# A two-block transformer kernel: attention steps, borders between stages, and the norm between two layers

## The reference

```python
for i in range(2):                                   # first block ("A")
    x = x + hybrid_mixer(rmsnorm(x, norm1_g[i]), w_in[i], ...) @ w_out[i]
    x = x + conv_glu_ffn(rmsnorm(x, norm2_g[i]), w_up[i], conv_w[i], conv_b[i], w_down[i])
x = rmsnorm(x, final_g)
for l in range(2):                                   # second block ("B")
    mod = (silu(c) @ ada_w[l] + ada_b[l]).reshape(b, 3, 3, 1024)   # shift, scale, gate of 3 sub-layers
    y = swiglu(x * (1 + scale0) + shift0, ffn_w13[l, 0], ffn_w2[l, 0])
    x = layer_norm(ALPHA * x + 0.5 * (1 + gate0) * y, ln_g[l, 0], ln_b[l, 0])
    y = token_mixer(x * (1 + scale1) + shift1, w_in[l], w_out[l], ...)
    x = layer_norm(ALPHA * x + (1 + gate1) * y, ln_g[l, 1], ln_b[l, 1])
    y = swiglu(x * (1 + scale2) + shift2, ffn_w13[l, 1], ffn_w2[l, 1])
    x = layer_norm(ALPHA * x + 0.5 * (1 + gate2) * y, ln_g[l, 2], ln_b[l, 2])
```

## Time and profile before

| | |
|---|---|
| median of 3 runs | 1954.8 us (1954.37 to 1962.56) |
| profiled execution | 1956.14 us |
| its span | 1954.3 us |
| PE busy | 1859.0 us (95%), 12538 matmuls |
| DVE busy | 1357.1 us (69%) |
| ACT busy | 956.5 us (49%) |
| POOL busy | 98.9 us (5%) |
| mean granted TensorE clock | 0.984 |
| chain of work that ended last | PE 85%, DVE 8%, ACT 5%, issue 2%, DMA 1% |

### The profile page before, as it was taken

One profiled execution on the slowest core, in us unless ns is written; L12 is line 12 of the kernel. 1 busy time (PEld: TensorE's weight loads), 2 busy tenths in 40 slices (PEclk: granted clock), 3 DMA queues, 4 the chain that ended last, 5 costly groups with the idle time before them and its releaser, 6 DMA issues.

```text
span 1954.3 us, 31245 instructions
## 1 busy us (share of the span) xinstructions
PE 1859.0 (95%) x12538; PEld 1705.4 (87%) x12538; DVE 1357.1 (69%) x2149; ACT 956.5 (49%) x1421; POOL 98.9 (5%) x104
## 2 busy tenths in 40 slices
PE   7989999899899989999998999998999999999997
PEld 5878999788799989998987989997999888979997
DVE  4576878647678876677777777677666777865445
ACT  5665444556644455434655354435343664444432
POOL 0000000000000000000002201100000001400100
PEclk9999999899999999999999999998999999999999
DMA  7215777431377767774530257775775432035552
GB/s 268 80 64 198 297 278 271 177 118 66 130 268 292 278 234 282 279 278 174 180 123 23 93 212 285 285 277 211 293 283 200 153 131 85 1 130 195 194 204 76
DMA packets 54509, 374.42 MB, mean 192 GB/s; under 512 B 6016, under 2 KB 6656, under 8 KB 12800
## 3 DMA queue, kind: packets, MB, share of 16 engines
q1 hardware_dynamic: 51536, 361.98, 50.2%
q0 software_dynamic: 2304, 9.93, 1.4%
q10 hardware_dynamic: 560, 0.99, 0.2%
HBM read 371.83 MB, written 1.05 MB: 191 GB/s over the span
## 4 chain that ended last, share of the span: by engine, by line
PE 85%; DVE 8%; ACT 5%; issue 2%; DMA 1%; SPq 0%; ACTq 0%; DVEq 0%
PE bank L688 13%; PE bank L690 13%; PE bank L689 13%; PE bank L837 6%; PE bank L838 6%; PE bank L839 6%; PE bank L754 3%; PE bank L755 3%; PE bank L756 3%; DVE w_lo L1911 2%; PE bank L1297 2%; PE bank L1307 1%; ACT w_hi L1395 1%; PE bank L799 1%; PE bank L800 1%
## 5 line engine op out<-in xcount | busy, mean ns | idle before, releaser
L1911 DVE TENSOR_TENSOR w_lo<-raw,w_hi 128x2048 fp32r<-128x2048 f32 (+4 forms) x273 | 605.2, 2220 | 88.2 <-ACT w_hi L1395 88.0
L688 PE MATMUL bank<-hT_hi,w_hi 128*128 128x256 f32 x2304 | 654.1, 284 | 2.0 <-DVE scratch L2611 2.0
L689 PE MATMUL bank<-hT_lo,w_hi 128*128 128x256 f32 x2304 | 651.8, 283 | 0.0
L690 PE MATMUL bank<-hT_hi,w_lo 128*128 128x256 f32 x2304 | 651.8, 283 | 0.0
L1395 ACT ACTIVATE w_hi<-raw 128x2048 fp32r<-128x2048 f32 (+4 forms) x270 | 505.5, 1875 | 146.3 <-PE bank L839 116.2
L688 PEld LDWEIGHTS bank<-hT_hi,w_hi 128*128 128x128 f32 x2304 | 440.1, 191 | 8.9 <-issue 6.5
L689 PEld LDWEIGHTS bank<-hT_lo,w_hi 128*128 128x128 f32 x2304 | 440.2, 191 | 2.8 <-issue 0.5
L690 PEld LDWEIGHTS bank<-hT_hi,w_lo 128*128 128x128 f32 x2304 | 440.2, 191 | 0.2
L837 PE MATMUL bank<-w_hi,hid_hi 128*128 128x512 f32 x528 | 207.3, 393 | 3.8 <-DVE w_lo L1911 3.4
L838 PE MATMUL bank<-w_lo,hid_hi 128*128 128x512 f32 x528 | 206.8, 392 | 0.0
L839 PE MATMUL bank<-w_hi,hid_lo 128*128 128x512 f32 x528 | 205.9, 390 | 0.0
(11 more groups left out here) (400 smaller groups left out, 2391.7 us busy)
## 6 DMA issues: line engine op xcount, KB each, us to landing
raw<-in_wb SPq DMA_DIRECT2D x158, 1024.0 KB, 4.8
raw<-in_wa SPq DMA_DIRECT2D x94, 1024.0 KB, 4.9
scratch<-in_wm SPq DMA_DIRECT2D x72, 1024.0 KB, 7.0
raw<-in_wb SPq DMA_DIRECT2D x8, 940.0 KB, 4.5
raw<-in_wb SPq DMA_DIRECT2D x4, 936.0 KB, 4.6
lnw<-in_ln_g POOLq DMA_DIRECT2D x6, 512.0 KB, 4.5
lnw<-in_ln_b POOLq DMA_DIRECT2D x6, 512.0 KB, 5.4
scratch<-in_c SPq DMA_DIRECT2D x5, 512.0 KB, 3.7
```

Of the source, the lines that this page charges most:

```text
L688: nc.tensor.matmul(out, ah, bh, start=(i == 0), stop=False)
L689: nc.tensor.matmul(out, ah, bl, start=False, stop=False)
L690: last = nc.tensor.matmul(out, al, bh, start=False, stop=(i == n - 1))
L1911: return nc.vector.tensor_tensor(w_lo[:, slot, cols], raw[:, raw_slot, cols], w_hi[:, slot, cols].bitcast(F32), ALU.subtract)
```

## The change

It has three parts.

**B's attention steps.** The first matrices of heads 4 and 5 are joined into one set of double width (`FIRST`) and moved from behind `systems` into attention steps 3, 4 and 5. Scores of the first two units wait only for the system matrix of heads 4 and 5; the wait on the token features moves to the first values. The denominators of the mLSTM norm (three small instructions) stand in step 10, and the wide multiply (128x768) behind the last output, no longer in step n = 3 of the inverse loop. The low part of chunk `wout` + 1 is made in four quarters: two between the last outputs, two behind the multiply.

**A's borders.** At the start of each layer of A tiles are split by halves of k: k 0 to 3 of both rows, chunk 1's high and low part, and then k 4 to 7. At the border from layer 0 to layer 1 ACT makes chunk 1's high part first, DVE adds the last sum first, and row 0's transposes stand ahead of the sweep's last product. The last piece of `ada` of A's FFN goes behind the last feature. The high part of chunk `A_WIN` (first of the output projection) is made in quarters on ACT in attention steps 9 to 12, its low part on DVE in step 20. Row 1 of the second norm and of the final norm is written in two halves, with a wait for each.

**B's border.** Between B's two layers row 0 and row 1 are only normalized, as between sub-layers. Gain and bias of that norm go into layer 1's first modulation (three more 128x8 instructions on DVE), and eight POOL instructions (128x512) put them on x during layer 1's first FFN.

The diff, cut to its core:

```diff
 # PE
+                            if (i, half, f) == (1, 1, FT - 1) and turn_first is not None:
+                                turn_first()
...
-                pe.wait_ge(A["xn"], due(A, "xn", 2 * TT))
-                turn_tile(A, xn, 1, 2)
-                ffn(A, split + (A_WIN + A_WOUT), FT * l, 2)
+                turn_tile(A, xn, 1, 2, lambda bank: pe.wait_ge(A["xn"], due(A, "xn", 2 * TT + bank)))
+                ffn(A, split + (A_WIN + A_WOUT), FT * l, 2, turn_first=turn_next if l + 1 < DEPTH else None)
...
-                    turn_row(i, lambda half, i=i: pe.wait_ge(FIN["x"], TT * l + i + 1))
+                    if l == 0:
+                        turn_row(i, lambda half, i=i: pe.wait_ge(FIN["x"], TT) if i and half else pe.wait_ge(FIN[("x", "x_half")[i]], 1))
+                    else:
+                        turn_row(i, lambda half, i=i: pe.wait_ge(EDGE[f"nx{i}"], half + 1))
...
-                    if 2 <= u < MOBA_H + 2:
+                    if u < 2:
+                        pe.wait_ge(B["dmul"], due(B, "dmul", GDN_H - 1 + u))
+                    elif u < MOBA_H + 2:
...
-                pe.wait_ge(B["tm"], due(B, "tm", N_TOK))
-                pe.wait_ge(B["dmul"], due(B, "dmul", GDN_H))
 # POOL, layer 1, first FFN
+                        for j in range(8):
+                            row, i, half = j // 4, j // 2 % 2, j % 2
+                            cols = slice(half * 512, half * 512 + 512)
+                            pool.wait_ge(chunk_mm, l * B_N + S_A + NEW + 4 + 2 * j)
+                            if row:
+                                pool.wait_ge(FIN["x"], TT + j - 3)
+                            nc.gpsimd.tensor_tensor(x[:, i, cols], x[:, i, cols], lnw[:, row, cols], (ALU.mult, ALU.add)[row]
+                                                    ).then_inc(FIN["x"], 1)
 # ACT, layer 0 of A (first lines) and layer 1
-                    hi_tile(A, 0, 0, "g1")
+                    hi_tile(A, 0, 0, "g1", range(KH))
+                    hi_tile(A, 0, 1, "g1", range(KH))
+                    hi_a(1)
...
-                hi_tile(A, 0, 1, "g1")
-                hi_a(1)
+                    hi_a(1)
+                    act.wait_ge(A["x"], summed(l - 1, 1, 0))
+                    square(NEXT, 1, 0)
+                    half_mean(NEXT, 1, 6 * l + 4)
+                    hi_tile(A, 0, 0, "g1", range(0, 2))
...
+                for i in range(TT):
+                    hi_tile(A, 0, i, "g1", range(KH, KT))
...
-                hi_a(A_WIN)
+                    if 0 <= step - SPLIT_AT < 4:
+                        hi_quarter(step - SPLIT_AT)
 # DVE
+                if l:
+                    scale, shift = by_kind[:, 0, 1, :], by_kind[:, 0, 0, :]
+                    link(nc.vector.tensor_tensor(bshift[:, 0, :], sbp("ln_b")[:, 2 * KT:3 * KT], scale, ALU.mult))
+                    link(nc.vector.tensor_tensor(shift, shift, bshift[:, 0, :], ALU.add))
+                    link(nc.vector.tensor_tensor(scale, scale, sbp("ln_g")[:, 2 * KT:3 * KT], ALU.mult))
...
-                    lo_tile(A, 0, 0, "g1", range(0, 4))
                     sums(l - 1, 1, 1)
+                    lo_tile(A, 0, 0, "g1", range(0, 2))
                     plain_row(1, TT * l + 2, 2 * TT * l + 2)
-                    lo_tile(A, 0, 0, "g1", range(4, KT))
-                lo_tile(A, 0, 1, "g1")
-                for c in range(1, A_WIN - 1):
+                    lo_tile(A, 0, 0, "g1", range(2, KH))
+                    lo_a(1)
+                    lo_tile(A, 0, 1, "g1", range(KH))
+                for i in range(TT):
+                    lo_tile(A, 0, i, "g1", range(KH, KT))
+                for c in range(2, A_WIN - 1):
...
-                    dve.wait_ge(B["dmul"], due(B, "dmul", h + 1))
-                    v = xx[:, 2 * h:2 * h + 2, 1, :]
-                    link(nc.vector.tensor_tensor(v, sysT[:, h, :].rearrange("p (k n) -> p k n", n=P)[:, 0:3:2, :],
-                                                 const("lev0").unsqueeze(1).to_broadcast([P, 2, P]), ALU.mult))
-                    nc.vector.tensor_tensor(v, ident.unsqueeze(1).to_broadcast([P, 2, P]), v, ALU.subtract).then_inc(B["xinit"], 1)
-                    dve.wait_ge(B["xinit"], due(B, "xinit", h + 1))
-                    nc.vector.transpose(xx[:, 2 * h:2 * h + 2, 0, :], v).then_inc(B["xt"], 1)
+                    if h < GDN_H - 2:
+                        for part in range(3):
+                            first_matrices(h, part)
...
+                    if 0 <= step - MOBA_H + 1 < 3:
+                        first_matrices(len(FIRST) - 1, step - MOBA_H + 1)
...
+                    if step > NUB and step + 1 < NUB + B_LAGV:
+                        lo_quarter(B_S0["wout"] + 1, step - NUB - 1)
+                dve.wait_ge(B["o_ev"], due(B, "o_ev", NUB))
+                link(nc.vector.tensor_tensor(hc, hc, wide(hst2), ALU.mult))
...
-                for half in range(2):
-                    from_down(2, 1, half, split + (B_N + NEW))
-                second_statistics()
-                for i in range(TT):
-                    last_row(2, i)
+                    from_down(2, 1, 0, None)
+                    first_scale(2)
+                    from_down(2, 1, 1, split + (B_N + NEW))
+                    second_statistics()
+                    second_normal(2)
```

More of the change, by code:

```diff
@@ L450, in build @@
         V_CHUNK = max(c for c, (f, _, _) in enumerate(B_WIN) if F_LQ - 1 in f)
+        FIRST = [(h, 1) for h in range(GDN_H - 2)] + [(GDN_H - 2, 2)]
         B_LAGP, B_LAGT, B_LAGO, B_LAGV = 1, 2, 3, 4
@@ L815, in gate_on_all, with ffn @@
                                      start=True, stop=True).then_inc(B["gateb"], 1)
-            def ffn(N, split, h0, v, gate=None):
+            def ffn(N, split, h0, v, gate=None, turn_first=None):
                 def up(f, f2, pos, slot, wait_bank=True, features=None):
@@ L1621, in compressed, with hi_quarter @@
                                              ACT.Copy).then_inc(A["cpt_ev"], 1)
+                def hi_quarter(q):
+                    s_, cols = A_WIN, slice(q * CW // 4, (q + 1) * CW // 4)
+                    if q == 0:
+                        act.wait_ge(raw_in[(s_ + A_D) % RING], arrivals(l, s_ + A_D))
+                        act.wait_ge(chunk_mm, split + s_ + 1)
+                    last = nc.scalar.activation(w_hi[:, s_ % RING, cols], raw[:, (s_ + A_D) % RING, cols], ACT.Copy)
+                    if q == 3:
+                        last.then_inc(hi_done, 1)
                 for step in range(NU + LAG_T):
@@ L2022, in ffn @@
                 post(FT - 1, 1, 1, lambda: None)
+                if conv:
+                    ada(turns - 1, 5)
                 if more and conv:
@@ L2334, in final_row @@
                 normed(NEXT, TT * DEPTH + i + 1, FIN, i + 1, i)
-                gained_row(i, x).then_inc(FIN["x"], 1)
+                if i == 0:
+                    gained_row(i, x).then_inc(FIN["x"], 1)
+                else:
+                    for half in range(2):
+                        cols = slice(half * 512, half * 512 + 512)
+                        nc.vector.scalar_tensor_tensor(out=x[:, i, cols], in0=x[:, i, cols], scalar=st[:, 20 + i:21 + i],
+                                                       in1=lnw[:, 0, cols], op0=ALU.mult, op1=ALU.mult
+                                                       ).then_inc(FIN[("x_half", "x")[half]], 1)
             dve.wait_ge(gain_in, 16 * DEPTH + 16)
@@ L2766, in _ @@
                     lo_rest(B_N, CW)
-                for half in range(2):
-                    from_down(2, 1, half, split + (B_N + NEW))
-                second_statistics()
-                for i in range(TT):
-                    last_row(2, i)
+                    from_down(2, 1, 0, None)
[3 more added lines that the diff above has]
+                    second_normal(2)
+                else:
+                    for half in range(2):
+                        from_down(2, 1, half, split + (B_N + NEW))
+                    second_statistics()
+                    for i in range(TT):
+                        last_row(2, i)
     return nc
```

140 lines of the change are left out of this document (96 added, 44 removed), and 1 row of the table B.

## The result

Sixteen runs of the changed kernel have a median of 1933.85 us (1927.15 to 1952.37), sixteen of the kernel before 1954.3 us. The ratio is 0.9889, 95% interval [0.9868, 0.991]: faster by 1.1%; the two medians lie 20.5 us apart. 1928 had been forecast, within a range of 1919 to 1942. The profiled execution took 1934.75 us with a span of 1932.9, against 1956.14 and 1954.3.

A forecast was written before the change was run, and what follows sets the result against it. PE was busy 95% of the span, so time goes only where it idles or runs at its lower clock. Terms 3.4 + 2.7 + 5.2 + 1.3 + 9.5 + 4.5 = 26.6 off 1956.14 gave 1929.5, 1928 against the median; range 1919 to 1942.

The forecast's parts named there:

- the bound named at the start of A: Start of A: chunk 2's low part would be late, so chunk 1 ends at 28.3 to 29.4 instead of 32.78.
- Start: Start of A: chunk 1 is ready earlier and PE's wait before it goes; -3.4 us, bounds -1 to -4.5.
- Output projection and second norm: Both layers of A: the 0.97 entry wait goes and row 1's norm comes in halves; -2.7 us, bounds -4 to +1.
- Border of A's layers with `ada`: A's layer border: sweep ends 1.2 earlier, chunk 1's wait goes, a new 3.6 wait precedes the first product; -5.2 us.
- Border from A to B: Between A and B: half of 1.28 off the 2.50 wait and half of `ada`'s 1.22; -1.3 us, bounds 0 to -2.
- B's attention: Both layers of B: first logits come earlier and the inverse's wait goes; together -9.5 us, bounds -3 to -11.
- the 0.2 before the inverse: B's attention: charge per layer for the wide multiply now standing before the inverse loop; 0.2 us, at most 0.9.
- Border of B's layers: Between B's layers: the plain norm shortens the 10.7 us from sweep to first product; -4.5 us, bounds -2.8 to -5.1.
- the analogue: Behind the first FFN of the same B layer, where the norm is plain: 6.1 us, taken for B's layer border.
- stalls are moved: Rival: idle time wanders elsewhere, as at A's layer border, and the clock falls either way; gain 15.3, 1939.5 us; chance 0.20.
- GpSimd does get in VectorE's way: Rival: POOL instructions in B's layer 1 FFN and under the logits delay DVE and PE; slower, 1972 us; chance 0.03.
- The inverse's wait: Rival, B's inverse step 3: POOL's masking or PE's queue held it, not DVE; 6.3 us less gain, 1934; chance 0.10.

The follow-up runs named there:

- first_back: Changed kernel with the joined first matrices of heads 4 and 5 back behind the last system, none in steps 3 to 5; the execution took 1938.48 us.
- border_tiles_first: Changed kernel with row 0's four tiles and row 1's statistics before chunk 1 at A's layer border; median 1931.49 us, ratio 0.987 to the kernel before.
- norm_back: Changed kernel with the four mLSTM norm instructions put back into step 3 of the inverse loop; the execution took 1949.36 us.
- pool_more: Changed kernel with 32 more GpSimd multiplies in layer 1's first FFN of B, four ahead of each of the eight; the execution took 1961.69 us.
- fill_and_border: Changed kernel with the fillers of fill_waits, but for 24 before A's layer 1, and the order of border_tiles_first; median 1922.82 us, ratio 0.9826 to the kernel before.
- fill_waits: Changed kernel with unread transposes of the identity in TensorE's waits; median 1920.65 us, ratio 0.9855 to the kernel before.

## Why the prediction was right, and where it was off

The median lay 5.85 us above the forecast, inside the range, and the mechanism of every part held but for the bound named at the start of A. The edits won 27.3 us where 26.6 had been forecast; 5.9 us lost elsewhere made 21.4 of it. Several sizes came out right by errors that cancel, as said below.

- *Start:* 3.1 of 3.4, partly by luck. The wait before chunk 1 is gone. The forecast took 29.4 for the end of chunk 1, from a low part of chunk 2 that would be late. That part was ready at 28.3 (26.04 + 2.29) and TensorE did not wait for it. What held chunk 1 until 29.69 was the clock: from 15.8 us on the matmuls of 128x512 came 0.43 us apart until 21.5, in the kernel before only until 18.6. (The windows say 1.00 there, so the sum of lost time leaves this out.) In `first_back`, where they came at full pace, TensorE waited 0.44 us before chunk 2, so there the bound is real.
- *Output projection and second norm:* 1.8 of 2.7. In layer 0 the 0.97 us were won and given back at once, since the clock was at half for the turn ahead of it (1.7 us lost at 140 to 146 us).
- *Border of A's layers with `ada`:* 6.1 of 5.2. The new wait, forecast at 3.6, came at 3.64, and half clock followed it (1.7 us lost, 1.9 counted). Moving `ada` was counted at 1.22 and is worth 1.8, and in this execution the half clock behind the old wait as well.
- *Border from A to B:* 1.3 of 1.3, by luck. The halved norm took 2.50 to 2.33 only, not 0.64 off, and the clock fell for the turn behind it (1.78 us instead of 1.09); from the sweep's end to the first product 0.2 us were won. The rest, 1.1, came ahead of the sweep's end, where `ada` was, of which half of 1.22 had been counted.
- *B's attention:* 11.0 of 9.5. The charge of 0.45 a layer for the steps was nothing, and so was the 0.2 before the inverse: from the last value product to the inverse's first matmul it is 3.06 us in both kernels. Undone, the inverse's part costs 4.1 us a layer, in layer 0 too, where 2.1 had been forecast: the half clock behind the wait comes or does not.
- *Border of B's layers:* 4.0 of 4.5. The first product comes 6.3 us behind the sweep, where the analogue had 6.1. The half clock named as its risk came for the second turn alone: it takes 1.94 us at a granted clock of 0.52. The first takes 1.36 at 1.00, as it does with the fillers. The kernel before had both at half (1.97 each).
- *Rivals:* "stalls are moved" is refuted at the start, the inverse and B's border. At A's border the wait did wander from before chunk 1 to before chunk 0, with half clock behind it both times, and yet the part gave 6.1 us and not the 1 that the rival left it. GpSimd does get in VectorE's way, but reaches TensorE at 40 instructions and not at 8, and without half clock behind it. Under the logits the second of the first matrices, 1.37 us beside a masking, takes 0.68 in its step (at 1033.50) though it is twice as wide; back behind the systems it takes 1.64. The inverse's wait was VectorE's.
- *Sums:* a chunk of 24 at full clock takes 5.45 us (0.227 a matmul), not 5.2. The better bounds of all parts add up to 33.6, not to the 36 from which the lower end of the range was taken.

The step that fell short is the first one: "The change touches about a dozen such places and no steady stage; the number of matmuls stays." The sum took from it that nothing happens elsewhere. In the profiled execution 5.9 us went to places without an edit, 4.5 of them behind layer 0's inverse. And 6 of 16 runs lie at 1938 us or more. Four other traces show the long stretch in A's attention: `border_tiles_first` (1938.53), `norm_back` (1949.36), `pool_more` (1961.69, twice) and, with fillers elsewhere, `fill_and_border` (1927.18). That these six have it too is argued from their mean clock (0.975 to 0.983, against 0.989 in the best run), since no profile of them was taken. The missing term is TensorE's clock away from the edits. It is also where most of the next 15 us were: the fillers alone bring the kernel from 1933.85 to 1920.65, and with the border's order and the fillers in A's attention it is 1918.96.

Whether the change makes that stretch more frequent is not settled. Of the 16 runs before, 3 lie over 1960 us (1961.97, 1962.56, 1974.38), and of the 29 beside the experiments 4 more; none of those was profiled.

## What to carry to other kernels

Price a stall with its idle time and with the half clock behind it, and then look at the granted clock of the stages that no edit touches, since it can come out differently there without a change of code or waits. Why it does is open here. Where TensorE waits 0.5 to 4 us for small work on other engines, transposes of a constant into a bank that is overwritten next held the clock and won 0.7% (1933.85 to 1920.65). The spread of the runs fell from 25 us to 13 by them, and to 2 only with more of them in A's attention. A wait put down to "issue" at the one step of a loop that has extra instructions on another engine was that engine's queue.

## What the runs showed of the hardware

- TensorE was busy 22.00 of 22.00 us at a granted clock of 0.51, among matmuls of 128x30 and 128x64, where other executions of the same code ran at 1.00 (busy 19.69 of 22 us).
- The same instructions behind the same waits (0.78 and 0.57 us) ran at 0.56 in one kernel and at 1.00 in another. What the clock does depends on more than the waits just before.
- Transposes of a constant in TensorE's waits held the granted clock at 1.00 until its last matmul (`fill_waits`).
- VectorE's two-input instructions and GpSimd's made each other 1.0 to 1.1 us longer (2.29 to 3.38 us, 1.3 to 2.3).
